# Two transformer blocks on one core: order of the hybrid layer's front and of the RWKV chunk queries

## The chip, the cores and the metric

The kernel runs on one NeuronCore of a Trainium2 chip. The metric is the device time of one execution in microseconds; the kernel before was timed three times, and one further execution was profiled.

## The reference

A first block of two layers and a second block of one layer work on 512 tokens of width 1024, with 256 context (later memory) rows beside them, all in float32. The change touches two places.

The first is the front of layer 0, the hybrid mixer:

```
mod = silu(c) @ ada_w + ada_b                      # six blocks of 1024 per layer
hx = rms_norm(x) * (1 + sc1) + sh1;  hc the same with the context's shift and scale
p = h @ w_in                                       # q, k, v, z, xbc, dt for 512 + 256 rows
q, k = rope(rms_norm(q)), rope(rms_norm(k))        # the context's k is not rotated
a = softmax(q k^T / 8) v                           # 8 heads, 2 key heads, 768 keys
xbc = silu(conv3(xbc) + conv_b)                    # 768 channels, width 3 along the tokens
dt = softplus(p_dt + bias);  y = ssd scan(xbc, dt) in both directions
out = [a, rms_norm(y * silu(z))] @ w_out
```

The second is the RWKV-7 recurrence of the second block, 16 heads of 64, which the kernel computes in chunks of 64 tokens: a chunk's transition matrix G and its own state H, the states S(c+1) = G S(c) + H, and the rows read from a state with the chunk's queries RQ.

## The kernel before

The program is one stream of instructions for each engine, written out by hand. Streams are tied by semaphores: a `Progress` object names the steps of one stream, `done("x")` is the count at which step x is over. Activations lie channel by partition: X, HX and the others hold 8 tiles of 128 channels by 512 tokens, the context's 256 behind them. Weights come as units of 512 KB through a ring of four slots that SyncE fills in one fixed order: it asks for unit u + 4 once TensorE has freed unit u. The `ada_w` rows go through four slots of their own (AW). The order of the streams decides everything around the change; no planner is involved.

The front of layer 0 runs so:

- VectorE sums the first two ada blocks (lines 2387 and 2398), TensorE adds them over the partitions (line 1131). VectorE norms the latent tiles (`norm_dve`, lines 778 and 787), then those of the context, then makes MOD, MODC and both GAINs (lines 2411 to 2415). ScalarE waits for the last of these, "gainc", and writes the latent and the context tiles of HX (line 684).
- Projections: for four query pairs and the key TensorE makes product, square sum (line 1171) and rope swap (line 1176), ScalarE copy, square and root, VectorE reciprocal and rotation (lines 2447 to 2455), and between them the first 12 ada units (line 2429). The value unit gives tokens by channels (line 1191).
- Attention: 16 steps g, four query tiles for each of four head pairs. TensorE's order in a step is `scores(g + 1)` (lines 1229, 1231), three eighths of a fill (line 1265), block sums of ada where a block has ended (line 1253), six transposes of head 0 (line 1242), two eighths of the fill, six transposes of head 1, the last three eighths, and behind each fourth step `values` (line 1280). A fill is one projection unit that attention doesn't need: z0 to z3, then xbc tile by tile, latent (512 columns) and context (256). ScalarE has `exps(g + 1)` (line 2057), two transposed copies (line 2070) and the fill's copy (line 2079). VectorE has `weights(g)` (lines 2491, 2493), `row_max(g + 1)` (line 2484) and five ada units, three in a step with a context fill.
- Tail: after the last values and the last block sum's MOD, VectorE convolves six tiles of 770 columns (lines 2517, 2520) into two buffers by turns, ScalarE takes SiLU of z (line 2085) and of each convolved tile (lines 2089, 2090), then exponential and logarithm for dt; TensorE transposes the convolved tiles (line 1306), VectorE makes dt (lines 2528 to 2556) and copies (line 2562). GpSimd fetches the B and C rows by DMA once the last tile is out. The scan over four head pairs follows.

In the RWKV part eight passes run, one for each head pair (`pair_pass`). After the inverse of a chunk TensorE makes the products for the queries ("rq", line 1648), the transitions ("gt", line 1653) and the states ("h", lines 1658, 1661). VectorE adds bonus (line 2890), queries (2893), transitions in two halves (2897), states (2901) and copies the first state (2904). Then six transitions follow, each one TensorE product (1680) and one VectorE step (2907), with products of the next pair's projections in between (1507).

Of the kernel before, what the change touches and what calls it, by code (L numbers as in the profile page):

```python
# [8 lines left out]
ALU = mybir.AluOpType  # L9
# [48 lines left out]
FILLS = [("z", j, U_Z + j) for j in range(NPAIR)] + [(part, j, U_X + j) for j in range(XBC_TILES) for part in ("lat", "ctx")]  # L58
# [4 lines left out]
for _kind, _, _ in FILLS:  # L63
    ADA_UPTO.append(ADA_UPTO[-1] + (3 if _kind == "ctx" else 5))
# [224 lines left out]
def two_blocks(nc, a, consts_d, bias_d, out):  # L289

    ctx = ExitStack()
    with ctx:
# [98 lines left out]
        t_cv = arena(low + 12900)  # L391
        CONV = t_cv(2, TA + 2)
# [85 lines left out]
        ada_dve = prog("ada_dve", "mod modc gain gainc")  # L478
        norm_lat, norm_ctx = NormStage(prog, "norm_lat", True), NormStage(prog, "norm_ctx", True)
        hy_act = prog("hy_act", "q0 sq0 q1 sq1 root0 k ksq root1 q2 sq2 kroot q3 sq3 root2 root3")  # L480
# [7 lines left out]
        at_act = prog("at_act", "exp00 exp01 " + by_step(lambda g: (f"exp{g + 1}0 exp{g + 1}1 " if g + 1 < STEPS else "") + f"pt{g}0 pt{g}1 e{g}"  # L488
# [43 lines left out]
        for steps, ahead in ((rw_steps, True), (rz_steps, False)):  # L532
            def next_pair(names):
# [4 lines left out]
                           + " w rq gt h s1 s2 yp s3 s4 s5 s6 y" + next_pair("lora") + "mean var")  # L538
# [7 lines left out]
                            + next_pair("nmax ninv nk") + "bv rq gt0 gt1 dh st1 s1 s2 s3 s4 s5 s6" + next_pair("d2 m2") + "ys yc"  # L546
# [320 lines left out]
        def _(sp):  # L867
# [257 lines left out]
        def _(pe):  # L1125
# [90 lines left out]
            nc.tensor.matmul(bank[4], const["rope_swap"], KT[:, 0:T], start=True, stop=True).then_inc(hy_pe.sem, hy_pe.step("kswap"))  # L1216
            swapped(2)
# [298 lines left out]
            def pair_pass(i, at, p_pe, p_act, p_dve, p_pool, ahead):  # L1516
# [129 lines left out]
                for t, c, e in quads:  # L1646
                    own = halves[c]
                    mm = nc.tensor.matmul(bank[2 + c][halves[e], t * CHUNK:(t + 1) * CHUNK], W21[own, 4 * e + t, 0, :], GR[own, 4 * e + t, 1, :], start=True, stop=True)
                mm.then_inc(p_pe.sem, p_pe.step("rq"))

                for t, c, e in quads:
                    own = halves[c]
# [9 lines left out]
                mm.then_inc(p_pe.sem, p_pe.step("h"))  # L1662

# [327 lines left out]
        def _(act):  # L1991
# [55 lines left out]
            query_root(2, "krstd")  # L2047
            query_root(3, "rstd2")
# [13 lines left out]
            for g in range(STEPS):  # L2062
# [13 lines left out]
                else:  # L2076
                    act.wait_ge(freed[ring.slot("hy_in", u)], ring.used("hy_in", u))
                    dst, src = (ZS[:, j, :], bank[7]) if kind == "z" else (XB[:, j, T + 3:TA + 3], bank[7][:, 0:TC])
                nc.scalar.activation(dst, src, ACT.Copy).then_inc(at_act.sem, at_act.step(f"e{g}"))
# [1045 lines left out]
```

## Time and profile before

| | us |
|---|---|
| median of the three timed runs | 2965.5 |
| the runs | 2955.92, 2965.5, 2968.95 |
| profiled execution, its own time | 2954.55 |
| its span | 2952.6 |
| TensorE matmul busy | 2752.6 (93%) |
| VectorE busy | 1709.6 (58%) |
| ScalarE busy | 645.8 (22%) |
| GpSimd busy | 188.5 (6%) |
| chain that ended last | TensorE 86%, VectorE 8%, issue 3% |
| mean granted clock of TensorE | 0.968 |

The span is the time from the first to the last recorded instruction; the execution's own time holds some 2 us more. The granted clock is a share of 2.4 GHz, so 0.50 is 1.2 GHz. Matmuls in float32 are recorded twice, so that one product of 128 by 512 shows as two records of 0.43 us.

### The profile page before, as it was taken

The numbers are of one execution on the slowest core, as the hardware profiler recorded it, in microseconds if no ns is written. First come the engines' busy times: TensorE is split into PE (matmuls) and PEld (weight loads), VectorE is DVE, ScalarE is ACT, GpSimd is POOL, SyncE is SP. The second block draws the span as 40 slices with busy tenths as digits, with TensorE's granted clock in tenths as the row PEclk, the third lists the DMA queues.
The fourth block names the chain that finished last, engine by engine and source line by source line (L and its number), as shares of the span: only waits on it lengthen the run. The fifth ranks groups of instructions, "written<-read, shape, count | busy, mean of one in ns | idle before, by whom it ended". The sixth has DMA issues, their size and how long they took to land.

```text
span 2952.6 us, 42986 instructions
## 1 busy us (share of the span) xinstructions
PE 2752.6 (93%) x17241; PEld 2007.0 (68%) x17241; DVE 1709.6 (58%) x2286; ACT 645.8 (22%) x1089; POOL 188.5 (6%) x203
## 2 busy tenths in 40 slices
PE   4799787999999999999989999998989999999998
PEld 3455443788887878888655555565557788788887
DVE  7677775655547665554456555663345575655554
ACT  3133412211101021110132223321341121211002
POOL 2000121000010010000030000010000010100001
PEclk8999898999999999999999999998999999999999
DMA  7466401333332323333211111111203333223332
GB/s 237 127 209 207 125 11 43 92 96 88 98 99 81 97 78 99 92 92 97 74 34 32 42 46 34 37 37 47 59 24 92 96 90 112 84 87 100 93 98 72
DMA packets 393989, 255.46 MB, mean 87 GB/s; under 512 B 19879, under 2 KB 376832, under 8 KB 393728
## 3 DMA queue, kind: packets, MB, share of 16 engines
q1 hardware_dynamic: 390256, 243.63, 28.0%
q0 software_dynamic: 2320, 5.11, 0.6%
q10 hardware_dynamic: 1280, 4.78, 0.4%
q8 instruction: 103, 1.69, 0.2%
q14 instruction: 30, 0.25, 0.0%
HBM read 250.60 MB, written 2.10 MB: 86 GB/s over the span
## 4 chain that ended last, share of the span: by engine, by line
PE 86%; DVE 8%; issue 3%; ACT 1%; DVEq 0%; DMA 0%; POOL 0%; ACTq 0%; SPq 0%; POOLq 0%
PE PS L827 14%; PE PS L826 14%; PE PS L828 14%; PE PS L1532 4%; PE PS L1507 3%; PE PS L841 3%; PE PS L842 3%; PE PS L843 3%; PE PS L813 3%; PE PS L1265 3%; PE PS L1598 1%; PE PS L1513 1%; PE PS L1624 1%; PE PS L1622 1%; PE PS L1718 1%
## 5 line engine op out<-in xcount | busy, mean ns | idle before, releaser
L852 DVE CAST WH<-W 128x1024 fp32r<-128x1024 f32 x304 | 213.3, 702 | 417.7 <-PE PS L828 371.9
L827 PE MATMUL PS<-XNL,WH 128*128 128x512 f32 x960 | 382.0, 398 | 0.0
L854 DVE TENSOR_TENSOR WL<-W,WH 128x1024 fp32r<-128x1024 f32 x304 | 374.5, 1232 | 10.4
L826 PE MATMUL PS<-HH,WH 128*128 128x512 f32 x672 | 262.3, 390 | 0.1
L827 PE MATMUL PS<-HL,WH 128*128 128x512 f32 x672 | 261.7, 389 | 0.0
L828 PE MATMUL PS<-HH,WL 128*128 128x512 f32 x672 | 261.7, 389 | 0.0
L827 PEld LDWEIGHTS PS<-XNL,WH 128*128 128x128 f32 x960 | 181.0, 189 | 41.5 <-issue 0.5
L828 PE MATMUL PS<-XNH,WL 128*128 128x512 f32 x512 | 201.7, 394 | 0.0
L826 PE MATMUL PS<-XNH,WH 128*128 128x512 f32 x512 | 201.2, 393 | 0.0
L826 PE MATMUL PS<-XN2H,WH 128*128 128x512 f32 x448 | 178.7, 399 | 10.7 <-issue 6.8
L828 PE MATMUL PS<-XN2H,WL 128*128 128x512 f32 x448 | 177.7, 397 | 0.0
L1532 PE MATMUL PS<-HXF,W 128*128 128x512 f32 x336 | 165.4, 618 | 0.0
L841 PE MATMUL PS<-XNH,WH 128*128 128x512 f32 x384 | 154.7, 403 | 9.9 <-DVE XNL L768 9.9
L842 PE MATMUL PS<-XNL,WH 128*128 128x512 f32 x384 | 154.9, 403 | 0.0
L843 PE MATMUL PS<-XNH,WL 128*128 128x512 f32 x384 | 153.6, 400 | 0.0
L826 PEld LDWEIGHTS PS<-HH,WH 128*128 128x128 f32 x672 | 126.1, 188 | 27.9 <-DVE HL L3092 1.3
L828 PEld LDWEIGHTS PS<-HH,WL 128*128 128x128 f32 x672 | 126.2, 188 | 26.4
L827 PEld LDWEIGHTS PS<-HL,WH 128*128 128x128 f32 x672 | 126.2, 188 | 26.1
L2880 DVE TENSOR_TENSOR ARENA<-ARENA,PS 128x512 f32<-128x512 f32 (+1 forms) x80 | 50.8, 635 | 140.2 <-PE PS L1624 139.9
L826 PEld LDWEIGHTS PS<-XNH,WH 128*128 128x128 f32 x512 | 96.4, 188 | 23.6 <-issue 0.2
L828 PEld LDWEIGHTS PS<-XNH,WL 128*128 128x128 f32 x512 | 96.2, 188 | 21.9
L826 PEld LDWEIGHTS PS<-XN2H,WH 128*128 128x128 f32 x448 | 85.1, 190 | 34.6 <-issue 14.7
(499 smaller groups left out, 4727.3 us busy)
## 6 DMA issues: line engine op xcount, KB each, us to landing
ARENA<-in_ada_w SPq DMA_DIRECT2D x80, 512.0 KB, 4.9
W<-in_ffn_w SPq DMA_DIRECT2D x64, 512.0 KB, 3.8
W<-in_w_in SPq DMA_DIRECT2D x51, 512.0 KB, 4.1
W<-in_ffn_w_gate SPq DMA_DIRECT2D x44, 512.0 KB, 3.8
W<-in_ffn_w_up SPq DMA_DIRECT2D x44, 512.0 KB, 3.8
W<-in_ffn_w_down SPq DMA_DIRECT2D x32, 512.0 KB, 3.7
W<-in_sc_w_in SPq DMA_DIRECT2D x24, 512.0 KB, 3.7
W<-in_ada_w SPq DMA_DIRECT2D x16, 512.0 KB, 4.7
```

Source lines behind the costliest of these rows:

```text
L813: mm = nc.tensor.matmul(dst, w[:, k, :], rhs(k), start=(start and k == 0), stop=(stop and k == kts - 1))
L826: nc.tensor.matmul(dst, WH[:, h, c], hi(k), start=(start and k == 0), stop=False)
L827: nc.tensor.matmul(dst, WH[:, h, c], lo(k), start=False, stop=False)
L828: mm = nc.tensor.matmul(dst, WL[:, h, c], hi(k), start=False, stop=(stop and k == kts - 1))
L841: nc.tensor.matmul(dst[u], WH[:, h, c], hi(k), start=(k == 0), stop=False)
L842: nc.tensor.matmul(dst[u], WH[:, h, c], lo(k), start=False, stop=False)
L843: mm = nc.tensor.matmul(dst[u], WL[:, h, c], hi(k), start=False, stop=(k == KD - 1))
L852: nc.vector.tensor_copy(WH[:, h, :], W[:, s, 0:D]).then_inc(parted, 1)
L854: nc.vector.tensor_tensor(WL[:, h, :], W[:, s, 0:D], WH[:, h, :], ALU.subtract).then_inc(freed[s], 1)
L1265: mm = nc.tensor.matmul(bank[7][:, 0:n], tiles(s)[:, k, :], (cx if kind == "ctx" else lat)(k), start=(k == 0), stop=(k == KD - 1))
L1507: return nc.tensor.matmul(bank[7], w, xn(k), start=(k == 0), stop=(k == KD - 1))
L1532: mm = nc.tensor.matmul(bank[7], tiles(s)[:, k, :], xn(k), start=(k == 0), stop=(k == KD - 1))
```

## The change

- The latent MOD and GAIN are made ahead of the context's norm, and ScalarE's latent outputs wait for that gain alone; the context's MODC and GAIN follow, then the context's norm.
- The first z unit is multiplied within the projections, behind the key's swap, into bank 2; ScalarE copies it out ahead of the last root. The list of fills begins with z1, all fills move up by one step, and step 15 has none. The first three eighths of step 0's fill stand ahead of `scores(1)`.
- The convolution of tile j runs on VectorE in step 5 + 2j, behind the maximum of the next step and ahead of the ada units. It writes into a buffer of its own (tile 0) or into the part of XB that tile j - 1 has left. These odd steps have three ada units, the others five; these were also the steps with three before.
- After attention ScalarE waits for the last MOD, takes SiLU of the six convolved tiles, and then SiLU of z.
- In each RWKV pair the "rq" matmuls go behind "h", and the add into RQ behind the copy of the first state.

```diff
-FILLS = [("z", j, U_Z + j) for j in range(NPAIR)] + [(part, j, U_X + j) for j in range(XBC_TILES) for part in ("lat", "ctx")]
+FILLS = ([("z", j, U_Z + j) for j in range(1, NPAIR)] + [(part, j, U_X + j) for j in range(XBC_TILES) for part in ("lat", "ctx")]
+         + [(None, None, None)])
+CONV_STEP = {5 + 2 * j: j for j in range(XBC_TILES)}
...
-for _kind, _, _ in FILLS:
-    ADA_UPTO.append(ADA_UPTO[-1] + (3 if _kind == "ctx" else 5))
+for _g in range(STEPS):
+    ADA_UPTO.append(ADA_UPTO[-1] + (3 if _g in CONV_STEP else 5))
...
-        t_cv = arena(low + 12900)
-        CONV = t_cv(2, TA + 2)
+        CONV = [t_hy(TA + 2)] + [XB[:, j, 0:TA + 2] for j in range(XBC_TILES - 1)]
...
         SyncE, per step: the z and ctx units of FILLS[g - 1] ask for unit u + 4
-                for u in [SLOTS + u for kind, _, u in FILLS[max(g - 1, 0):g] if kind != "lat" and SLOTS + u < 16]:
+                for u in [SLOTS + u for kind, _, u in (FILLS[g - 1:g] if g else [("z", 0, U_Z)]) if kind in ("z", "ctx") and SLOTS + u < 16]:
...
         TensorE, after the key's swap
+            s = ring.slot("hy_in", U_Z)
+            pe.wait_ge(hy_act.sem, hy_act.done("sq2"))
+            pe.wait_ge(landed[s], ring.arrived("hy_in", U_Z))
+            unit_product(pe, "hy_in", U_Z, 0, bank[2], lat, KD).then_inc(freed[s], 1)
             swapped(2)
...
         TensorE, fill(g, ks)
+                if kind is None:
+                    return
...
+                    else:
+                        pe.wait_ge(hy_dve.sem, hy_dve.done("sin3"))
...
             pe.wait_ge(hy_dve.sem, hy_dve.done("dt"))
+            pe.wait_ge(hy_act.sem, hy_act.done("z0"))
             scores(0)
             for g in range(STEPS):
+                if g == 0:
+                    fill(g, range(0, 3))
                 if g + 1 < STEPS:
                     scores(g + 1)
-                fill(g, range(0, 3))
+                if g:
+                    fill(g, range(0, 3))
...
         TensorE, RWKV pair: the rq loop (its four lines unchanged) goes from ahead of gt to behind h
...
         ScalarE
+            act.wait_ge(ada_dve.sem, ada_dve.done("gain"))
+            norm_act_out(act, norm_lat, HX[:, :, 0:T], GAIN[:, 0, :], MOD[:, 0:KD])
             act.wait_ge(ada_dve.sem, ada_dve.done("gainc"))
-            norm_act_out(act, norm_lat, HX[:, :, 0:T], GAIN[:, 0, :], MOD[:, 0:KD])
             norm_act_out(act, norm_ctx, HX[:, :, T:TA], GAIN[:, 1, :], MODC[:, 0:KD])
...
             query_root(2, "krstd")
+            act.wait_ge(freed[ring.slot("hy_in", U_Z)], ring.used("hy_in", U_Z))
+            nc.scalar.activation(ZS[:, 0, :], bank[2], ACT.Copy).then_inc(hy_act.sem, hy_act.step("z0"))
             query_root(3, "rstd2")
...
-            act.wait_ge(at_act.sem, at_act.done(f"e{NPAIR - 1}"))
-            nc.scalar.activation(ZS, ZS, ACT.Silu).then_inc(zs_act.sem, zs_act.step("silu"))
             act.wait_ge(at_dve.sem, at_dve.done(f"p{STEPS - 1}1"))
+            act.wait_ge(blocks_dve.sem, blocks_dve.done(f"b{len(ADA_BLOCKS) - 1}"))
             for j in range(XBC_TILES):
                 act.wait_ge(cv_dve.sem, cv_dve.done(f"c{j}"))
                 (the two Silu activations read CONV[j] instead of CONV[:, j % 2])
+            act.wait_ge(at_act.sem, at_act.done(f"e{NPAIR - 2}"))
+            nc.scalar.activation(ZS, ZS, ACT.Silu).then_inc(zs_act.sem, zs_act.step("silu"))
...
         VectorE
             norm_dve(dve, norm_lat, X, HX[:, :, 0:T], T)
             dve.wait_ge(norm_lat.dve.sem, norm_lat.dve.done(f"n{KD - 1}"))
-            norm_dve(dve, norm_ctx, CX, HX[:, :, T:TA], TC)
...
+            for m, at, name, step in ((MOD, 0, "mod", "gain"), (MODC, 4 * N_MOD, "modc", "gainc")):
+                nc.vector.tensor_tensor(m[:, 0:16], two(at, 16), adab(0, 16), ALU.add).then_inc(ada_dve.sem, ada_dve.step(name))
+                dve.wait_ge(ada_dve.sem, ada_dve.done(name))
+                nc.vector.scalar_tensor_tensor(GAIN[:, 0 if m is MOD else 1, :], m[:, KD:2 * KD], 1.0, cols_of("norm_mix", 0, KD), ALU.add, ALU.mult).then_inc(ada_dve.sem, ada_dve.step(step))
+            norm_dve(dve, norm_ctx, CX, HX[:, :, T:TA], TC)
...
+            def convolution(j):
+
+                dve.wait_ge(at_act.sem, at_act.done(f"e{4 + 2 * j}"))
+                out_ = CONV[j]
+                (the loop over "abc" as it was; from j = 2 on a waits for c of tile j - 1)
...
             for g in range(STEPS):
                 weights(g)
                 if g + 1 < STEPS:
                     row_max(g + 1)
+                if g in CONV_STEP:
+                    convolution(CONV_STEP[g])
                 for n in range(ADA_UPTO[g], ADA_UPTO[g + 1]):
                     ada_unit(n)
...
-            dve.wait_ge(at_pe.sem, at_pe.done(f"pv{NPAIR - 1}"))
-            dve.wait_ge(at_act.sem, at_act.done(f"e{STEPS - 1}"))
-            for j in range(XBC_TILES):
-                (wait for ScalarE's silu of tile j - 2, then the loop over "abc" into CONV[:, j % 2])
...
         VectorE, RWKV pair: the wait for rq and the add into RQ go from behind bv to behind st1
```


## Rows read from the trace of the kernel before

**Rows 1.** The page, part 1: busy us, share, instructions of each engine.
```profile
PE 2752.6 (93%) x17241; PEld 2007.0 (68%) x17241; DVE 1709.6 (58%) x2286; ACT 645.8 (22%) x1089; POOL 188.5 (6%) x203
```

**Rows 2.** Busy time by stretch; columns: stretch, length, five engines, TensorE clock, DMA.
```profile
60.00:66.00 6.00, 0.00 (x0) 0.00 (x0) 5.46 (x17) 0.45 (x1) 0.00 (x0) 0.50 0.20 79
336.50:353.70 17.20, 0.03 (x1) 0.03 (x1) 16.25 (x23) 7.90 (x14) 0.00 (x0) 0.58 0.00 0
```

**Rows 3.** Timeline, norms to query 0; columns: start us, length, instruction, idle time before, releaser.
```profile
60.51 1.75 DVE L778 RECIPROCAL RSTD<-ROOT 128x256 f32<-128x256 f32 x1
...
65.55 5.75 ACT L684 ACTIVATE HXF<-HXF,MOD,GAIN 128x512 f32<-128x512 f32 x8 [9.51 <-DVE GAIN L2415]
...
66.50 15.42 PE L813 MATMUL PS<-HXF,W 128*128 128x512 f32 x32 [7.13 <-ACT HXF L684]
```

**Rows 4.** Timeline of SyncE and TensorE, late projections.
```profile
108.03 0.43 SPq L891 DMA_DIRECT2D W<-in_hy_w_in  x1
...
129.53 2.07 PE L1176 MATMUL PS<-ARENA,CONST 128*128 128x512 f32 x2 [8.80 <-DVE ARENA L2449]
```

**Rows 5.** Timeline of TensorE, first steps of attention.
```profile
152.29 2.08 PE L1229 MATMUL PS<-ARENA 64*128 64x512 f32 x4 [4.30 <-ACT ARENA L2057]
...
155.15 4.33 PE L1265 MATMUL PS<-HXF,W 128*128 128x512 f32 x6
```

**Rows 6.** Timeline of TensorE, then VectorE, steps 8 to 10 of attention.
```profile
260.05 1.13 PE L1229 MATMUL PS<-ARENA 64*128 64x512 f32 x4
...
265.36 0.85 PE L1242 MATMUL PS<-CONST,ARENA 128*128 128x128 f32 x6 [0.74 <-ACT ARENA L2070]
...
267.43 1.13 PE L1229 MATMUL PS<-ARENA 64*128 64x512 f32 x4
...
279.04 1.13 PE L1229 MATMUL PS<-ARENA 64*128 64x512 f32 x4
...
250.05 1.82 DVE L2484 TENSOR_REDUCE ARENA<-PS 128x1 f32<-128x768 f32 x2 [5.44 <-PE PS L1231]
...
263.39 4.05 DVE L2429 SCALAR_TENSOR_TENSOR ARENA<-ARENA,SILU_C 128x1024 f32<-128x1024 f32 x3
...
267.56 0.62 DVE L2493 TENSOR_SCALAR ARENA<-ARENA 128x768 f32<-128x768 f32 x1
```

**Rows 7.** Timeline of the tail: TensorE, VectorE, ScalarE.
```profile
328.38 5.37 PE L1280 MATMUL PS<-ARENA 128*64 128x512 f32 x24
334.44 1.95 PE L1253 MATMUL PS<-CONST,ARENA 128*128 128x2 f32 x16 [0.70 <-ACT ARENA L2082]
353.68 5.38 PE L1306 MATMUL PS<-CONST,ARENA 128*128 128x128 f32 x24 [17.28 <-ACT ARENA L2090]
...
336.51 0.62 DVE L2517 TENSOR_SCALAR ARENA<-ARENA,COLS 128x770 f32<-128x770 f32 x1
...
355.43 0.21 DVE L2536 TENSOR_SCALAR ARENA<-ARENA 128x96 f32<-128x96 f32 x1 [2.17 <-ACT ARENA L2096]
...
335.70 1.91 ACT L2085 ACTIVATE ARENA<-ARENA 128x2048 f32<-128x2048 f32 x1
...
352.50 0.72 ACT L2089 ACTIVATE ARENA<-ARENA,COLS 128x512 f32<-128x512 f32 x1 [1.52 <-DVE ARENA L2520]
353.13 0.49 ACT L2090 ACTIVATE ARENA<-ARENA,COLS 128x256 f32<-128x256 f32 x1
```

**Rows 8.** Timeline of the second RWKV pair: VectorE, then TensorE.
```profile
1624.06 0.69 DVE L2893 TENSOR_TENSOR ARENA<-PS,ARENA 128x512 f32<-128x512 f32 x1
1624.67 1.40 DVE L2897 TENSOR_TENSOR ARENA<-PS,CONST 64x512 f32<-64x512 f32 x2
...
1626.83 0.20 DVE L2904 COPY ARENA<-ARENA 128x64 f32<-128x64 f32 x1
...
1627.17 0.41 PE L1680 MATMUL PS<-ARENA 128*128 128x64 f32 x2 [1.77 <-DVE ARENA L2904]
...
1629.12 1.91 PE L1507 MATMUL PS<-HXF,W 128*128 128x512 f32 x2
```

More of the change, by code:

```diff
@@ L537, in two_blocks @@
                                       + (" akv" if l == 0 else "") for l in levels)
-                           + " w rq gt h s1 s2 yp s3 s4 s5 s6 y" + next_pair("lora") + "mean var")
+                           + " w gt h rq s1 s2 yp s3 s4 s5 s6 y" + next_pair("lora") + "mean var")
             steps["act"] = (("raw0" if ahead else "dila") + " tr0 tr1 tr2 tr3 "
@@ L1647, in pair_pass @@
                     own = halves[c]
[L1648 to L1652, printed above, removed]
                     mm = nc.tensor.matmul(bank[4 + c][halves[e], t * HEAD:(t + 1) * HEAD], W21[own, 4 * e + t, 0, :], TOK[own, t, 1, halves[e]], start=True, stop=True)
@@ L1662, in pair_pass @@
                 mm.then_inc(p_pe.sem, p_pe.step("h"))
+                for t, c, e in quads:
+                    own = halves[c]
+                    mm = nc.tensor.matmul(bank[2 + c][halves[e], t * CHUNK:(t + 1) * CHUNK], W21[own, 4 * e + t, 0, :], GR[own, 4 * e + t, 1, :], start=True, stop=True)
+                mm.then_inc(p_pe.sem, p_pe.step("rq"))
                 def inside_rows(tiles_of):
@@ L2410, in _ @@
             cols_of = lambda name, k, n: COLS[:, COL[name] + k:COL[name] + k + n]
-            nc.vector.tensor_tensor(MOD[:, 0:16], two(0, 16), adab(0, 16), ALU.add).then_inc(ada_dve.sem, ada_dve.step("mod"))
-            nc.vector.tensor_tensor(MODC[:, 0:16], two(4 * N_MOD, 16), adab(0, 16), ALU.add).then_inc(ada_dve.sem, ada_dve.step("modc"))
-            dve.wait_ge(ada_dve.sem, ada_dve.done("modc"))
-            for w, m in enumerate((MOD, MODC)):
-                nc.vector.scalar_tensor_tensor(GAIN[:, w, :], m[:, KD:2 * KD], 1.0, cols_of("norm_mix", 0, KD), ALU.add, ALU.mult).then_inc(ada_dve.sem, ada_dve.step(("gain", "gainc")[w]))
+            for m, at, name, step in ((MOD, 0, "mod", "gain"), (MODC, 4 * N_MOD, "modc", "gainc")):
[3 more added lines that the diff above has]
+            norm_dve(dve, norm_ctx, CX, HX[:, :, T:TA], TC)
             dve.wait_ge(norm_ctx.dve.sem, norm_ctx.dve.done(f"n{KD - 1}"))
@@ L2493, in weights @@
                     nc.vector.tensor_scalar(PR[g % 2][:, e, :], PR[g % 2][:, e, :], own, None, ALU.mult).then_inc(at_dve.sem, at_dve.step(f"p{g}{e}"))
+            def convolution(j):
+                dve.wait_ge(at_act.sem, at_act.done(f"e{4 + 2 * j}"))
+                out_ = CONV[j]
+                for w, step in enumerate("abc"):
+                    src, wcol = XB[:, j, w:w + TA + 2], col("conv_w", w * XBC_TILES + j)
+                    if w == 0:
+                        if j > 1:
+                            dve.wait_ge(cv_dve.sem, cv_dve.done(f"c{j - 1}"))
+                        ins = nc.vector.tensor_scalar(out_, src, wcol, None, ALU.mult)
+                    else:
+                        dve.wait_ge(cv_dve.sem, cv_dve.done(f"{'abc'[w - 1]}{j}"))
+                        ins = nc.vector.scalar_tensor_tensor(out_, src, wcol, out_, ALU.mult, ALU.add)
+                    ins.then_inc(cv_dve.sem, cv_dve.step(f"{step}{j}"))
             row_max(0)
@@ L2890, in pair_pass @@
                 tt(BV, bank[6], v, ALU.mult).then_inc(p_dve.sem, p_dve.step("bv"))
-                dve.wait_ge(p_pe.sem, p_pe.done("rq", at))
-                by_chunk = lambda ap: ap.rearrange("p t (c d) -> p t c d", c=2)
-                tt(by_chunk(RQ), chunk_pairs(2), by_chunk(AR[:, :, 1, :]), ALU.add).then_inc(p_dve.sem, p_dve.step("rq"))
                 dve.wait_ge(p_pe.sem, p_pe.done("gt", at))
@@ L2904, in pair_pass @@
                 nc.vector.tensor_copy(ST[:, 1, :], DH[:, 0, :]).then_inc(p_dve.sem, p_dve.step("st1"))
+                dve.wait_ge(p_pe.sem, p_pe.done("rq", at))
+                by_chunk = lambda ap: ap.rearrange("p t (c d) -> p t c d", c=2)
+                tt(by_chunk(RQ), chunk_pairs(2), by_chunk(AR[:, :, 1, :]), ALU.add).then_inc(p_dve.sem, p_dve.step("rq"))
                 for c in range(1, NCHUNK - 1):
```

28 lines of the change are left out of this document (9 added, 19 removed).

## The prediction

> **What bounds the kernel now.** I read the busy line first: TensorE is busy 93% of the span, VectorE 58% [rows 1]; the chain that ended last is TensorE's to 86%. So an edit pays only where TensorE stands idle and waits for the work that is moved, or where work leaves a stretch in which TensorE sets the pace. The table by stretches shows two such places at once: 60 to 66 us, no matmul, and 336.5 to 353.7 us, 17.2 us with one matmul, VectorE busy 16.25 us [rows 2]. The timelines then show what runs there, and three smaller gaps: 8.80 us ahead of the third query's swap, 4.30 us ahead of the second scores, and 1.77 us in each RWKV pair [rows 4, 5, 8]. One clock fact colours all: after an idle stretch TensorE comes back at a granted 0.50, that is 1.2 GHz; the same four score matmuls take 2.08 us then and 1.13 us at 2.4 GHz [rows 5, 6].
>
> The sum is made against the profiled execution, 2954.55 us (span 2952.6 and some 2 us around it). The three timed runs have their median at 2965.5, 11 us above it, so I subtract the same sum from the median.
>
> **A. Gain of the latent rows ahead of the context's norm.** Today the latent tiles are normed when the reciprocal of the context starts at 60.51; ScalarE's latent outputs start at 65.55, once the context's reciprocal, eight products and four small adds are through, and query 0 follows at 66.50 [rows 3]. In the new order MOD and GAIN (two small adds, some 0.35 us with their waits; TensorE's sums, their input, ended before 60 [rows 2]) stand directly at 60.51, so the outputs start at 60.9: 65.55 - 60.9 = 4.65 us. The context's norm then ends at 65.6 and its outputs go through ScalarE from 66.6 to 70.6; the key product that needs them comes after two queries (15.4 us from 61.85), at 78. Up to the first scores everything hangs on this chain of TensorE and VectorE, so all moves by **4.65**.
>
> **B. First z unit in the projections.** Sixteen matmul records of 0.43 us are 6.9 us. They stand between the key's swap (ends 129.53 - 8.80 = 120.7) and swap 2, which waits for VectorE until 129.53 [rows 4]: hidden, if the weights are there; SyncE asks for that unit at 108.03 [rows 4] and such 512 KB land in some 4 us. The copy by ScalarE (0.6 us) stands ahead of root 3, whose input comes later. If the cover were gone it would cost 6.9. The gap filled, swap 2 runs at 2.4 GHz: 2.07 becomes 1.1, and the next VectorE step waits for just it: **0.95** (bounds 0 and 0.95).
>
> **C. The fills move up by one.** (1) Step 0. The first three k of the fill (six records, 4.33 us at the low clock) now stand before scores 1 instead of behind, in the 4.30 us in which TensorE waits for the exponentials [rows 5]. They hide. Scores 1 then come after busy time: 3.0 us at the low clock become 1.5. Together 4.3 + 1.4 = **5.7** (4.3 if the clock stays low).
> (2) Full steps. From scores to scores a step with a 512-column fill takes 11.6 us with block sums (9.9 without their 1.7), one with a 256-column fill 7.4, of which 0.9 is waiting (8.2 without the wait and with block sums), values 5.3 [rows 6, 7]. Until now VectorE had three ada units (1.33 each) in the short steps; the trace shows TensorE waiting 0.74 us there for ScalarE's transposed copy, behind maximum and exponentials [rows 6]. Now the odd steps have the long fill, three units and a convolution (six take 336.51 to 352.4, 2.65 us each [rows 7]), the even ones five units, short fill and block sums. VectorE's pair, from start to next start: two weights of 1.44 (reciprocal and product, twice), two maxima of 1.74, eight units 10.1, mod 0.1, convolution 2.65: 19.25 us [rows 6, 7]. TensorE's pair: 9.9 + 8.3 = 18.2. VectorE lags, but the values (5.3 us, no VectorE work) let it catch up once in four steps. Walked through four steps with these durations, maximum g+1 starts 1.3 us late in the second step and 2.2 late in the fourth, and TensorE waits 0.1, 0.45 and 0.85 us for the copy: 1.4 in place of 1.8 (0.9 twice). Two such groups: **0.8** (bounds -5, if the pair's whole excess of 1 us is paid in five pairs, and 3.6, all waits gone).
> (3) Last four steps. Step 15 has no fill. TensorE's work is 6.9 us less, but the last pair is VectorE's: its weights come 29.6 us after scores 13, transposes and copies end at 32.7, values at 38.0, against 42.0 today. That is 4.0. Behind the last fill stand some 3 us of idle time and only transposes, and rows say what idle costs: values (5.37) and block sums (1.95) [rows 7] at 1.2 GHz would take up to 7 more. I take 3, left **1.0** (bounds -3 and 4).
>
> **D. Convolution out of the tail.** Today: last block sum taken over at 336.5, six convolutions to 352.4, last SiLU at 353.62, transposes at 353.68 [rows 7]. After: all convolutions lie in attention (the last in step 15, under values), and ScalarE starts when the last mod is there: table load 1.28, six times 1.03 (0.72 and 0.49 pipelined), so transposes 7.5 us after it instead of 17.2: 9.6. But SiLU of z (1.91) now stands behind them on the same engine, ahead of the dt exponentials. VectorE waits for that exponential even today, 2.17 us [rows 7]; it comes 1.9 later relative to the transposes. Its chain (dta, three copies) then reaches the C.B products at 8.6 us behind the last SiLU instead of 7.5. So 1.1 is given back: **8.5** (bounds 7.5 and 9.6). The B and C copies by DMA start when the last tile is out and are wanted 7 us later. What waits behind ScalarE's new wait for the last mod is only this work.
>
> **E. RWKV.** Today the chunk query matmuls (32 records, 0.52 us issue) and their add on VectorE (0.69, next start 0.61 later) lie before the transition adds; state 1 comes at 1626.83 and the first transition at 1627.17, TensorE idle 1.77 [rows 8]. Behind h the matmuls fall into that idle time, and the adds start with the transition at 1624.06, its products having been where the queries' were. State 1 comes 0.61 earlier. The query add then fills the 0.6 us in which VectorE waits for transition 1. From there TensorE is busy without a gap to the pair's end, so eight pairs give 8 x 0.61 = **4.9** (bounds 0 and 5).
> The clock there: in four of seven projecting pairs it falls to 1.2 GHz some 2 us behind that idle time (two records take 1.91 us [rows 8], elsewhere 1.08), and state 1 to y takes 10.6 instead of 8.96 us, 1.7 more. Idle time of 1.2 instead of 1.8 us may spare some or none: I take one, **1.7** (bounds -5, dips in all seven, and 6.8, none).
> The Trainium skill, "TensorE: Matmul & The Clock Gate", part "A second HAM failure mode: psum-queue depth-cycling", says that small idle times between groups of matmuls are enough to make the clock swing. The trace agrees (four of seven). By it alone, fewer idle times mean fewer dips, 6.8 for E in place of 1.7; and against C it speaks, as the last rival does.
>
> **Sum.** 4.65 + 0.95 + 5.7 + 0.8 + 1.0 + 8.5 + 4.9 + 1.7 = 28.2. Profiled execution 2926.3; median 2965.5 - 28.2 = 2937.
>
> **Rivals.**
> 1. VectorE becomes the bound of attention. For: 19.25 against 18.2 us a pair, and ScalarE between them. Against: VectorE stands idle 5.44 us at each values [rows 6]. If the five convolutions beside fills are paid in full, 5 x 2.65 = 13.3 lost: 2950.
> 2. The idle stretches are not removed but refilled: a later link (weights of an earlier asked unit, the dt chain on ScalarE, scores 0) sets the pace, and of A to D, 21.6 us, half is seen: 2948. For: each gap has a second releaser close behind (dt chain 1.1). Against: those that I could follow come later only by what is subtracted.
> 3. More: no dip in RWKV and values at the full clock: 28.2 + 5.1 + 3 = 36: 2929.
> 4. Slower. The waits for VectorE in steps 5 to 14 grow until the clock falls to 1.2 GHz in every step. Ten steps have 83 us of matmul time at 2.4 GHz and as much again at 1.2: 2937 + 83 = 3020, half of it 2978. It decides from idle times about as long as the 1.77 us after which RWKV shows dips; I come to 0.85. That swing of the clock is what the named page of the Trainium skill speaks of.
>
> **Chances.** Forecast 0.60, rival 3 0.15, rival 1 0.10, rival 2 0.10, rival 4 0.05. Leaving out rival 4 and the far ends, and with 5 us for the spread of the runs, the range is 2918 to 2955. A measurement of this kernel can tell some 0.5%, 15 us, from no change. Faster by more than that (below 2950.7): forecast and rival 3 nearly whole, half of 1 and 2: 0.83. Within: 0.13. Slower: 0.04.
>
> **What would show it.** Latent outputs near 60.9; no idle time ahead of swap 2; scores 1 under 2 us and at the old wait's end; the wait for the transposed copy under 1 us in steps 5 to 14; values 3 at 5.3 or up to 10.6 us; transposes 7.5 us after the last mod; first transition 1.2 us after h in every pair. Wrong would make it: the clock below 1.0 between steps 2 and 14, or VectorE busy without a gap through the values.

## The result and the profile after

| | before | after |
|---|---|---|
| median of the runs, us | 2966.25 (4 runs) | 2934.94 (4 runs) |
| profiled execution, us (span) | 2954.55 (2952.6) | 2924.85 (2922.9) |
| mean granted clock of that execution | 0.968 | 0.971 |

The ratio of the times, changed to before, is 0.9907, 95% interval 0.9889 to 0.9925: 22 to 33 us less. The forecast was 28.2 us less and a median of 2937. In the page of the changed kernel, TensorE's busy time hardly moves against [rows 1]; what went is idle time.

```profile
PE 2748.7 (94%) x17241; PEld 2005.4 (69%) x17241; DVE 1707.1 (58%) x2286; ACT 644.9 (22%) x1089; POOL 187.1 (6%) x203
```

The timelines of the changed kernel answer to the rows in their order (start, length, instruction, idle time before it and its releaser). The front, ScalarE and then TensorE, answers to [rows 3, 4]: the latent outputs start at 61.05 instead of 65.55, query 0 at 62.01 instead of 66.50, and swap 2 takes 1.18 instead of 2.07 us, with 1.94 us of idle time ahead of it instead of 8.80.

```profile
61.05 5.75 ACT L685 ACTIVATE HXF<-HXF,MOD,GAIN 128x512 f32<-128x512 f32 x8 [4.87 <-DVE GAIN L2430]
...
62.01 16.68 PE L814 MATMUL PS<-HXF,W 128*128 128x512 f32 x32 [2.50 <-ACT HXF L685]
...
101.55 1.86 PE L1209 MATMUL PS<-ARENA,CONST 128*128 128x512 f32 x2
...
119.00 7.03 PE L814 MATMUL PS<-HXF,W 128*128 128x512 f32 x16
127.97 1.18 PE L1177 MATMUL PS<-ARENA,CONST 128*128 128x512 f32 x2 [1.94 <-DVE ARENA L2464]
```

TensorE in attention answers to [rows 5 to 7]: the fill of step 0 stands ahead of the second scores (149.85), which now run at 2.4 GHz (1.13 instead of 2.08 us). In the middle the longest wait for the transposed copy is 0.62 us, where it was 0.74. In the last step, now without a fill, waits of 2.67, 0.99 and 0.95 us stand ahead of both groups of transposes and of values 3, which takes 6.99 instead of 5.37 us.

```profile
145.48 3.07 PE L1274 MATMUL PS<-HXF,W 128*128 128x512 f32 x6
149.85 1.13 PE L1234 MATMUL PS<-ARENA 64*128 64x512 f32 x4 [1.31 <-ACT ARENA L2072]
150.82 0.60 PE L1236 MATMUL PS<-ARENA 64*128 64x256 f32 x4
151.34 1.95 PE L1258 MATMUL PS<-CONST,ARENA 128*128 128x2 f32 x16
...
264.73 0.85 PE L1247 MATMUL PS<-CONST,ARENA 128*128 128x128 f32 x6 [0.18 <-ACT ARENA L2085]
...
274.13 0.85 PE L1247 MATMUL PS<-CONST,ARENA 128*128 128x128 f32 x6 [0.62 <-ACT ARENA L2085]
...
312.43 0.88 PE L1247 MATMUL PS<-CONST,ARENA 128*128 128x128 f32 x6 [2.67 <-DVE ARENA L2508]
...
314.29 1.51 PE L1247 MATMUL PS<-CONST,ARENA 128*128 128x128 f32 x6 [0.99 <-ACT ARENA L2085]
316.75 6.99 PE L1289 MATMUL PS<-ARENA 128*64 128x512 f32 x24 [0.95 <-issue]
324.43 1.95 PE L1258 MATMUL PS<-CONST,ARENA 128*128 128x2 f32 x16 [0.69 <-ACT ARENA L2098]
```

The tail (TensorE, VectorE, ScalarE) answers to [rows 7]. The transposes of the convolved rows wait 7.79 us instead of 17.28, and now for ScalarE's SiLUs alone. The SiLU of z (334.02) stands behind them, and VectorE waits 10.36 us for ScalarE's exponential, which comes after it.

```profile
334.16 4.26 PE L1319 MATMUL PS<-CONST,ARENA 128*128 128x128 f32 x24 [7.79 <-ACT ARENA L2105]
...
346.23 3.78 PE L1372 MATMUL PS<-ARENA,CONST 128*128 128x512 f32 x4 [1.39 <-ACT ARENA L2124]
...
326.41 0.17 DVE L2455 TENSOR_TENSOR MOD<-PS,COLS 128x8 f32<-128x8 f32 x1 [6.70 <-PE PS L1258]
...
337.72 0.21 DVE L2553 TENSOR_SCALAR ARENA<-ARENA 128x96 f32<-128x96 f32 x1 [10.36 <-ACT ARENA L2113]
...
326.64 1.28 ACT L2104 ACT_TABLE_LOAD   x1 [2.27 <-DVE MOD L2455]
...
333.62 0.49 ACT L2105 ACTIVATE ARENA<-ARENA,COLS 128x256 f32<-128x256 f32 x1
334.02 1.90 ACT L2107 ACTIVATE ARENA<-ARENA 128x2048 f32<-128x2048 f32 x1
```

The second RWKV pass, VectorE and then TensorE, answers to [rows 8]: the query add stands behind the copy of state 1, the idle time ahead of the first transition is 1.17 instead of 1.77 us, and the first late projection takes 1.12 instead of 1.91. From state 1 to the next pass's state 1 it is 65.45 us in each of the first six passes; before it was 66.05 or 67.7. A pass in which the clock falls to 1.2 GHz behind the idle time, and state 1 to y takes longer for it, is called one with a dip below.

```profile
1605.69 0.20 DVE L2918 COPY ARENA<-ARENA 128x64 f32<-128x64 f32 x1
1605.80 0.69 DVE L2921 TENSOR_TENSOR ARENA<-PS,ARENA 128x512 f32<-128x512 f32 x1
...
1606.03 0.41 PE L1692 MATMUL PS<-ARENA 128*128 128x64 f32 x2 [1.17 <-DVE ARENA L2918]
...
1607.99 1.12 PE L1520 MATMUL PS<-HXF,W 128*128 128x512 f32 x2
```

### The profile page after: what moved, and what is told of

It reads as the page before. It is cut to its first block, busy times and chain, and to the rows that moved or that the text cites. A ratio compares the mean times of both kernels' runs of the same rounds, so it can differ in the third digit from the quotient of the medians.

```text
span 2922.9 us, 42991 instructions
## 1 busy us (share of the span) xinstructions
PE 2748.7 (94%) x17241; PEld 2005.4 (69%) x17241; DVE 1707.1 (58%) x2286; ACT 644.9 (22%) x1089; POOL 187.1 (6%) x203
## 4 chain that ended last, share of the span: by engine, by line
PE 83%; DVE 9%; issue 4%; ACT 2%; POOL 1%; DMA 1%; DVEq 0%; ACTq 0%; POOLq 0%; SPq 0%
PE PS L828 14%; PE PS L827 14%; PE PS L829 14%; PE PS L1545 4%; PE PS L1520 3%; PE PS L843 3%; PE PS L842 3%; PE PS L844 3%; PE PS L814 2%; DVE ARENA L2444 2%; PE PS L1611 2%; PE PS L1637 1%; PE PS L1526 1%; PE PS L1635 1%; PE PS L1274 1%
## 5 line engine op out<-in xcount | busy, mean ns | idle before, releaser
L855 DVE TENSOR_TENSOR WL<-W,WH 128x1024 fp32r<-128x1024 f32 x304 | 374.5, 1232 | 10.4
```

The lines of the kernel that those rows point to most:

```text
L855: nc.vector.tensor_tensor(WL[:, h, :], W[:, s, 0:D], WH[:, h, :], ALU.subtract).then_inc(freed[s], 1)
```

## The experiments

The study is told in the order of its questions. Letters are the prediction's terms. Runs of one kernel spread over 3 to 16 us, so each comparison has a time and a place in the trace. Ratios are to the kernel before, run beside the version, with a 95% interval in brackets.

**RWKV order alone** (the kernel before, with part E and nothing else):

```
TensorE's order, then VectorE's
- " w rq gt h s1 s2 ..."
+ " w gt h rq s1 s2 ..."
- "bv rq gt0 gt1 dh st1 s1 ..."
+ "bv gt0 gt1 dh st1 rq s1 ..."
```

> The kernel before with the RWKV reorder alone. First theory (the sum's term E): TensorE's idle time ahead of the first transition goes from 1.77 to 1.17 us in each of eight passes, 8 x 0.61 = 4.9 us, and with the shorter idle time the clock falls in fewer of the seven projecting passes than the four of before, down to none as in the changed kernel's profile, up to 6.8 us more: passes 65.45 us apart throughout, time 5 to 12 us under the kernel before, ratio 0.996 to 0.998. Rival: the falls of the clock belong to the execution and not to the idle time; then some passes still stand 67.1 us apart, and the gain is 4.9 us, ratio 0.998.

Measured: 2948.03 us, median of 10 runs; ratio 0.9966 [0.9952, 0.9981], 6 to 14 us less, 10 in the middle. The idle time ahead of the first transition is 1.17 or 1.18 us in each pass, as in the changed kernel:

```profile
1629.96 0.41 PE L1679 MATMUL PS<-ARENA 128*128 128x64 f32 x2 [1.18 <-DVE ARENA L2900]
```

State 1 to y took 10.65 us in one of seven projecting passes and 8.96 to 9.13 in the others; in the kernel before it was four of seven. So E is worth about 10 us, more than the 6.6 taken, and the excess is the dips. The rival, that they belong to the execution and not to the idle time, needs the count over all profiles, further on.

**Front alone** (the changed kernel with RWKV's old order, the reverse of the diff above):

> The changed kernel with the RWKV part as before (queries ahead of the transitions in both streams). First theory: all of A to D stays, some 18 to 21 us under the kernel before (ratio 0.993 to 0.994), the idle time in RWKV is 1.77 us again and some passes show the clock at 1.2 GHz, so passes stand 66.06 or 67.7 us apart. Rival (the falls of the clock belong to the execution): passes all 66.06 us apart may come as often as not; then the profile shows no dip although the idle time is 1.77 us.

Measured: 2944.14 us; ratio 0.9957 [0.9941, 0.9974], 8 to 17 us less. Five of seven passes have the dip, with 1.77 us of idle time as before. The two halves, 10.1 and 12.7 us, sum to 22.8 against 27.5 for both; the intervals allow that they simply add. The front alone came out below its expectation and below the trace (19 us, in the table further on); its own runs go from 2937.2, the profiled one, to 2947.1, and why three of four were longer by 5 to 10 us no trace shows.

**Latent gain first, alone** (the kernel before, with part A):

```
- norm_dve(dve, norm_ctx, ...)      (stood ahead of both gains)
+ mod gain modc gainc, then norm_dve(dve, norm_ctx, ...)
```

> The kernel before with term A alone, the latent gain ahead of the context's norm. First theory: the latent outputs start 4.5 us earlier (65.55 to 61.05) and everything behind shifts rigidly, so scores 0 come at 140.6 instead of 145.06, ratio 0.9985. Rival, from the changed kernel's profile, where scores 0 came only 2.4 us earlier: the head start is partly paid back by stretches at 1.2 GHz in the projections (query 0 and the key's square sums), whose place moves with the start, so scores 0 come at 142 to 143.5 and the ratio is 0.999.

Measured: 2952.74 us (10 runs); ratio 0.9980 [0.9970, 0.9990], 3 to 9 us less. In its trace query 0 came at 61.83 (4.67 us earlier than [rows 3]), but the first scores at 143.28 against 145.06, 1.8 us earlier, as the rival said. A second trace of the kernel before shows how much of that gap is chance:

**The kernel before, once more**

> The kernel before, unchanged, for a second profile. Its first scores stood at 145.06 us in the first one. The versions with the changed front put them at 142.4 to 142.8 in four profiles and at 139.3 and 139.9 in two, with a granted clock from 60 to 80 us of 0.81 to 0.82 in the late and 0.87 to 0.88 in the early ones. Theory that the gap is scatter of the clock and not of the change: this profile has the scores at 142 to 143 or at 145, whichever, and dips in 3 to 5 of its seven full RWKV passes. Rival, that the change itself brings the low stretches at 66 to 120 us: 145.06 again within 0.3.

Measured: 2969.54 us (one run), first scores at 147.36, dips in five of seven. This is neither of the two places that the expectation named: the first profile's 145.06 was itself early (the RWKV-only kernel, with the same front, had 147.37). The key's square sums tell the two kinds of execution apart. In the first profile of before the longer of them ran at 2.4 GHz (1.02 us):

```profile
104.81 1.02 PE L1208 MATMUL PS<-ARENA,CONST 128*128 128x512 f32 x2
```

In the second it ran at 1.2 GHz (1.91):

```profile
105.87 1.91 PE L1208 MATMUL PS<-ARENA,CONST 128*128 128x512 f32 x2
...
147.36 2.08 PE L1229 MATMUL PS<-ARENA 64*128 64x512 f32 x4 [2.80 <-DVE ARENA L2475]
```

In the version with A alone it did so too:

```profile
101.33 1.92 PE L1208 MATMUL PS<-ARENA,CONST 128*128 128x512 f32 x2
...
143.28 2.08 PE L1229 MATMUL PS<-ARENA 64*128 64x512 f32 x4 [2.80 <-DVE ARENA L2474]
```

Like against like, A is worth 4.1 us at the first scores (147.36 - 143.28), near the 4.65 taken. Most of what seemed given back was the kind of execution that the first profile of before happened to be.

**Fill of step 0 behind the second scores again** (C1 undone):

```
-                if g == 0:
-                    fill(g, range(0, 3))
                 if g + 1 < STEPS:
                     scores(g + 1)
-                if g:
-                    fill(g, range(0, 3))
+                fill(g, range(0, 3))
```

> The changed kernel with the fill of attention step 0 put back behind the scores of step 1 (the term C1 undone; it was 5.7 us in the two traces, 3.1 of it the fill itself). My theory: the first block sums come 5 to 6 us later and so does every marker behind them, 5 to 6 us in the end (2940 to 2941). Rival: the fill itself is off the path, since the scores of step 1 wait for their PSUM anyway (idle 1.31 us ahead of them now): then 1.3 us of it comes back and the loss is about 4.3 us. Second rival: the 5.7 us came from the shorter scores (full instead of low clock in step 1) and not from the order; then the loss is under 2 us.

Measured: 2942.17 us, 6.5 above the 2935.6 that is the median of all ten runs of the changed kernel; its four runs go from 2932 to 2945, so it is the trace that decides. TensorE's timeline of step 0 gives the old picture back: 4.31 us of idle time, scores of 2.08 us, and the fill behind them.

```profile
142.40 2.08 PE L1234 MATMUL PS<-ARENA 64*128 64x512 f32 x4 [2.80 <-DVE ARENA L2487]
...
149.64 2.08 PE L1234 MATMUL PS<-ARENA 64*128 64x512 f32 x4 [4.31 <-ACT ARENA L2069]
...
152.50 4.24 PE L1274 MATMUL PS<-HXF,W 128*128 128x512 f32 x6
156.57 1.84 PE L1258 MATMUL PS<-CONST,ARENA 128*128 128x2 f32 x16
```

The block sums stand 14.17 us behind the first scores, in the changed kernel 8.72: 5.45. Both rivals, 4.3 and under 2, are out in the trace. (The expectation's 5.7 for the two traces is 5.54 by the starts of the block sums, see C1 below.)

**Convolutions behind the last modulation again** (D undone), run twice, the second time beside the changed kernel itself:

```
-                if g in CONV_STEP:
-                    convolution(CONV_STEP[g])
...
+            for j in range(XBC_TILES):
+                convolution(j)
```

> The changed kernel with the six convolution groups of the hybrid's attention put back behind the last modulation matmul, as before (the convolution's own term, D, undone; everything else as changed). My theory (D = 9.6 us off the tail, 1.1 us given back by a scan start that waits for the output gate): TensorE's tail transposes start about 17 to 18 us after the last MOD group instead of 7.8 us, and the kernel takes 8 to 10 us longer than the changed one (2943 to 2945, about 0.994 of before). Rival: the convolution had been hidden behind the last attention step in the old order as well (its matmuls fill idle time of TensorE there): then under 3 us longer. Second rival: with fewer matmuls in the last steps the clock is lower there and values 3 takes 8.2 instead of 7.0 us, which would add 1.2 us to the first.

> The changed kernel, unchanged, timed beside the next two. Scatter theory: its median lies at 2928 to 2937 and its first scores at 139.5 or at 142.6; no dip, or one, in the seven full RWKV passes (gaps of 65.45 us). It is the mark for the next two kernels.

> The kernel with the convolutions back behind the last modulation, again. In its first profile the tail's transposes stood 199.2 us behind the first scores against 191.5 in the changed kernel (7.6 us), but its median (2934.2) was no longer than that of the changed kernel (2934.9), measured in another call. Theory (the 7.6 us are real and scatter in the clock hid them): beside the changed kernel on one chip it takes 6 to 9 us more (0.2 to 0.3 per cent). Rival (given back later, in the scan, in the feed-forward layer or by the clock): no difference over 2 us.

Measured: first 2934.18 us (4 runs), as fast as the changed kernel's 2934.94, which was not run beside it. Side by side it took 2944.47 against 2935.77 (6 runs each; ratios 0.9936 [0.9919, 0.9952] and 0.9914 [0.9898, 0.9931]): 8.7 us by the medians, 6.5 by the ratios. Over all, ten runs each, the means are 2939.3 and 2934.2: 5.1 us, with a standard error of 2.5. By the times alone the part is only just clear of the spread; the traces say where it lies. The changed kernel's own second profile had its first scores at 142.55, as expected, but two dips where none or one was. TensorE, then VectorE, in the first trace of the version without the change:

```profile
306.93 0.88 PE L1247 MATMUL PS<-CONST,ARENA 128*128 128x128 f32 x6 [1.86 <-DVE ARENA L2508]
...
310.58 7.01 PE L1289 MATMUL PS<-ARENA 128*64 128x512 f32 x24 [0.95 <-issue]
318.28 1.95 PE L1258 MATMUL PS<-CONST,ARENA 128*128 128x2 f32 x16 [0.69 <-ACT ARENA L2098]
338.51 4.15 PE L1319 MATMUL PS<-CONST,ARENA 128*128 128x128 f32 x24 [18.27 <-ACT ARENA L2105]
...
335.22 2.08 DVE L2522 SCALAR_TENSOR_TENSOR ARENA<-ARENA,COLS 128x770 f32<-128x770 f32 x2
```

The idle time ahead of the transposes is 18.27 us against 7.79: the tail pays 10.5. But its first scores stood at 139.33, so its last block sums came 178.95 us behind them, against 181.81 in the changed kernel: without convolutions between VectorE's maxima, attention is 2.9 us shorter. There no wait for a transposed copy is left until the last step, and the wait for the last weights is 1.86 us instead of 2.67. Net 7.6 in this trace, 4.4 in the second, where values 3 took 5.37 against 7.89. The second rival (a longer values 3) was not seen: 7.01 and 5.37 us.

**More idle time in RWKV** (the changed kernel; VectorE's query add ahead of the transition adds, while TensorE's queries stay behind h):

```
- "bv gt0 gt1 dh st1 rq s1 ..."
+ "bv rq gt0 gt1 dh st1 s1 ..."
```

> The changed kernel with VectorE's query add back ahead of the transition adds, TensorE's query matmuls left behind h. VectorE now waits for the late matmuls, so the first state comes some 1.3 us later than in the kernel before and TensorE stands idle some 3.1 us ahead of the first transition. First theory: idle time decides the dips, so most or all of the seven passes show 1.2 GHz behind it (1.7 us each), passes some 69 us apart: against the changed kernel 8 x 1.9 + up to 7 x 1.7 = 15 to 27 us more, ratio to the kernel before 0.995 to 0.999. Rival (idle time doesn't decide): 15 us more than the changed kernel and no more than four dips, ratio 0.995 to 0.997 with passes 67.4 us apart mostly.

Measured: 2966.74 us; ratio 1.0025 [1.0009, 1.0042]. One of its six runs took 3563 us at a mean granted clock of 0.737 (0.962 to 0.964 in the others); the ratio leaves it out, it has no trace, and nothing here has a reason for it. TensorE's timeline:

```profile
1614.65 0.41 PE L1692 MATMUL PS<-ARENA 128*128 128x64 f32 x2 [3.17 <-DVE ARENA L2921]
...
1617.35 2.07 PE L1520 MATMUL PS<-HXF,W 128*128 128x512 f32 x2
```

The idle time is 3.17 us in each pass, and all seven have the dip (state 1 to y 10.5 to 12.2 us). Against the changed kernel's median of 2935.6 that is 31 us more, beyond the 15 to 27 expected: from the first state 1 to the eighth it is 30.3, of which 7 x 2.0 are the idle time and 16 are dips, up to 3.3 us each instead of 1.7. The rival (no more than four dips) is out.

**SiLU early** (a version meant to beat both; run twice). ScalarE loads the SiLU table right behind its last transposed copy and does SiLU of z and four convolved tiles there, two more behind the last output copy; nothing of it waits for the last modulation any more, only for the last use of the weights that lay where the tiles go.

```
+                if g == STEPS - 1:
+                    nc.scalar.activation(ZS, ZS, ACT.Silu)...
+                    for u in range(AW_SLOTS):
+                        act.wait_ge(aw_used[u], ADA_UNITS // AW_SLOTS)
+                    for j in range(4):
+                        conv_silu(j)
-            act.wait_ge(blocks_dve.sem, ...)
-            for j in range(XBC_TILES): ... (both SiLUs of tile j)
+            for j in range(4, XBC_TILES):
+                conv_silu(j)
```

> A version meant to go beyond the changed kernel: ScalarE runs the SiLU of z and of the first four convolution tiles right behind its last exponential and ahead of the last output copy, with the table load there, instead of behind the last modulation; the convolution groups are already there by then. In the changed kernel 7.75 us lie between the last MOD group's start (326.41) and the tail's transposes (334.16), and the transposes wait for the SiLU in that time. Theory: the transposes then start at about 326.7 to 328, 6 to 7.5 us earlier, the scan start no longer waits for the output gate (1.1 us), and the kernel takes 6 to 8.5 us less than the changed one (2926.5 to 2929). Rival: the copies that ScalarE owes to the attention's end come later by the table load and five SiLUs (about 1.3 + 6 us) and the last modulation with them, so that the gain is 0 to 2 us.

> The kernel with the SiLU early, again, with more rounds. In its first profile the tail's transposes stood 184.4 us behind the first scores against 191.5 (7.1 us), the start of hybrid output 321.6 us behind them against 323.8 (2.2 us only), and its median was 11.9 us below the changed kernel's of another call. Theory (7.1 us stay): 6 to 9 us less than the changed kernel in this call. Rival (5 us of them are given back ahead of the hybrid's output, by low clock or by a later wait in the scan): 1.5 to 3 us less.

Measured: 2923.06 us (4 runs), then 2927.62 (4 runs) beside the changed kernel's 2935.77; ratios to before 0.9866 [0.984, 0.9892] and 0.989 [0.9875, 0.9906]. Side by side that is 8.1 us less by the medians, 7.1 by the ratios. The timeline of TensorE in its first trace:

```profile
314.04 7.28 PE L1289 MATMUL PS<-ARENA 128*64 128x512 f32 x24 [0.95 <-issue]
322.00 1.95 PE L1258 MATMUL PS<-CONST,ARENA 128*128 128x2 f32 x16 [0.69 <-ACT ARENA L2112]
324.30 4.48 PE L1319 MATMUL PS<-CONST,ARENA 128*128 128x128 f32 x24 [0.35 <-DVE MOD L2463]
```

The wait of 7.79 us is 0.35, and the output copy that ScalarE owes is no later. The 7.4 us stay, and the rival (5 of them given back) is out. Its 2923.06 us is the lowest median of the study, though the next version is not told apart from it. Its first trace was only 2.2 us ahead at the hybrid's output: its stretch from the transposes to there took 137.22 us at a granted clock of 0.87, against 132.25 at 0.90, see the spread below.

**SiLU early and a fill of z in the last step** (the z unit taken from the third step, later fills up by one):

```
- FILLS = z1 z2 z3, 12 units of x, none
+ FILLS = z1 z2, 12 units of x, none, z3
  (each convolution waits for the fill one step earlier)
```

> As the kernel before in this call (SiLU early), and a projection unit of z moved from an early attention step to the last one as a fill, so that TensorE has matmuls beside its transposes there. Theory (values 3 took 6.99 us at the low clock in the changed kernel, 5.37 in the kernel before, where such matmuls stood there): values 3 takes 5.4 us and the transposes of the last step run without the low clock, 1.6 to 3 us less than with the SiLU early alone. Rival: the fill takes 2.1 to 3.1 us of TensorE's own time in a step where TensorE sets the end, and the sum is nought or a loss of 1 us; the SiLU of z waits for it as well.

Measured: 2927.11 us, against 2923.06 for the version before, run beside it; ratio 0.9885 [0.9857, 0.9914], so not told apart. TensorE:

```profile
303.98 1.92 PE L1258 MATMUL PS<-CONST,ARENA 128*128 128x2 f32 x16 [1.24 <-DVE ARENA L2452]
...
308.91 1.51 PE L1247 MATMUL PS<-CONST,ARENA 128*128 128x128 f32 x6 [1.91 <-ACT ARENA L2091]
...
319.83 5.37 PE L1289 MATMUL PS<-ARENA 128*64 128x512 f32 x24
```

Values 3 is at 2.4 GHz as expected. But the transposes stand 188.0 us behind the first scores, against 184.4 and 185.3: the step without a fill is now the last but one and waits there, and the fill costs its own time. The rival holds, with 2.7 to 3.6 us lost up to there where it named 1 at most; the total shows no more than that nothing is gained.

## Why the prediction was right, and where its terms were off

Each kernel's profile is cut at four places: the first scores, the tail's first transposes, the first matmul of hybrid output, the end. As several kernels share each stretch unchanged, means over them take out much of the chance (all in us; old order, then as changed; n is the number of profiles).

| stretch | old | changed | gain | forecast |
|---|---|---|---|---|
| start to first scores | 146.60 (n 3) | 142.04 (n 10) | 4.6 | A + B = 5.6 |
| first scores to transposes | 208.33 (n 4) | 192.21 (n 4) | 16.1 | C1 + C2 + C3 + 9.6 = 17.1 |
| transposes to hybrid output | 133.09 (n 4) | 134.43 (n 4) | -1.3 | -1.1 |
| hybrid output to the end | 2468.85 (n 4) | 2459.41 (n 9) | 9.4 | E = 6.6 |
| sum | | | 28.8 | 28.2 |

The forecast is right in its mechanism and near in its number; how near is partly luck, since misses of 1 to 3 us cancel. In the prediction's working some roundings are off by 0.1 us (a pair of TensorE's steps is 9.9 + 8.2, 17.2 - 7.5 is 9.7), and nothing hangs on them.

**A and B.** The mechanism held: query 0 4.49 us earlier (4.65 forecast), swap 2 0.89 shorter (0.95). The z unit's 7.03 us lie in the old gap; no run has B alone, so B is read from the traces. In the first pair of traces the scores gained 2.4 us only, since queries 0 and 1 took 1.3 us longer, and 1.7 us went in the key's two square sums and the product behind them, at 1.2 GHz from 101.6 us. But that pair compares unlike executions. Those sums ran at 1.2 GHz in nine of the eleven profiles with the new front and in two of the three with the old. Where they did, the first scores went from 147.37 to 142.65 us (two and eight profiles with both A and B), 4.7 less; where they did not, from 145.06 to 139.6 (one and two), 5.4 less. So of 5.6 forecast 0.2 to 0.9 is missing; all profiles together, mixed as they came, give 1.0.

**C1.** 5.7 forecast; 5.54 in the first pair of traces, and 5.45 with only this undone. The first block sums came 7.98 us earlier, of which 2.44 are the first scores'. They start at 151.34 in the changed kernel, and in the kernel before:

```profile
159.32 1.84 PE L1253 MATMUL PS<-CONST,ARENA 128*128 128x2 f32 x16
```

**C2.** 0.8 forecast, 1.1 found (values 0 7.87 us earlier, values 2 8.95). The undoing of D shows it to be a difference of two larger sizes: the convolutions cost 1.4 us up to values 2 and 2.9 to the last block sums, so the rest of the change there gives 2.5 up to values 2. That it is the ada units, now three beside a long fill and five beside a short one, is argued and not shown: no run moved them alone. Rival 1, VectorE as the bound with 13.3 us lost, is refuted as a size and real as a mechanism. Rival 4 is refuted: from 160 to 320 us the granted clock is 0.98 to 1.00 in the ten traces compared.

**C3.** 1.0 forecast and 1.1 found in the first pair (the last block sums 10.01 us earlier), with 1.6 of the 3 us set aside for the low clock in values 3. That clock is chance: values 3 took from 5.37 to 8.21 us, and two profiles of one kernel gave 6.99 and 7.89, 7.01 and 5.37, 7.28 and 5.37. All lie within the bounds, none at the far one of 10.6.

**D.** Transposes 7.79 us behind the last modulation's sums (7.5 forecast, 17.28 before), 1.1 given back behind it (the products at 346.23 stand 12.07 us behind the transposes, before it was 10.92). Right in the pair of traces. As a price of the part by itself 8.5 was too high, since C2 paid 2.9 of it: undone alone, it is 4.4 to 7.6 us in the traces.

**E.** The term that was mis-sized. "I take one" dip less; in fact nearly all went. Over all profiles the dips in the seven projecting passes are these:

| idle time ahead of the first transition | profiles | passes with the dip |
|---|---|---|
| 1.17 us (new order) | 9 | 4 of 63 |
| 1.77 us (old order) | 4 | 19 of 28 |
| 3.17 us (add ahead, queries behind) | 1 | 7 of 7 |

From the first state 1 to the eighth, the old order takes 468.2 us and the new one 457.8, 10.4 less (four and nine profiles). Behind the eighth 1.2 us is given back. "From there TensorE is busy without a gap" holds for seven passes only: the eighth has no late projections, and TensorE waits 0.38 us ahead of each transition from the fourth on, in either order. But the query add costs nothing there: the first transition step starts 0.79 us behind the copy of state 1 in either order. What differs is the clock of the y product. It took 1.97 us in eight of the nine profiles of the new order:

```profile
2003.05 1.97 PE L1703 MATMUL PS<-ARENA 64*64 64x64 f32 x32 [0.38 <-DVE ARENA L2924]
```

In the ninth, the RWKV-only kernel, it took 1.15, as in three of four of the old order:

```profile
2027.84 1.15 PE L1690 MATMUL PS<-ARENA 64*64 64x64 f32 x32 [0.38 <-DVE ARENA L2906]
```

That accounts for 0.5 of the 1.2 us by the means; the rest lies behind y, and its cause is open. The Trainium skill, "TensorE: Matmul & The Clock Gate", part "A second HAM failure mode: psum-queue depth-cycling", says of another kernel that small idle times between its groups of matmuls make the clock swing. The trace agrees, and by it alone E would have been 4.9 + 6.8 = 11.7, against 9.4 measured; no row of before could tell how fast the swing vanishes between 1.77 and 1.17 us.

So 28.2 was near because E was 3 us too small while A with B, and C with D, were 1 us too large each. Rival 2 (gaps refilled, half the gain of 21.6) is refuted by the first three stretches, which give 19.4; rival 3 was half right, in its dips but not in values at the full clock.

**The spread.** The same instructions of the scan, from the transposes to hybrid output, in windows (stretch, length, busy time of TensorE, its weight loads, VectorE, ScalarE, GpSimd, then granted clock, DMA share and GB/s): the kernel before twice, and the version with convolutions behind twice.

```profile
353.68:483.99 130.31, 101.30 (x461) 58.73 (x461) 97.77 (x240) 29.72 (x53) 25.63 (x24) 0.91 0.05 15
```

```profile
355.55:494.73 139.18, 109.46 (x461) 63.16 (x461) 97.78 (x240) 29.74 (x53) 26.06 (x24) 0.86 0.05 14
```

```profile
338.51:470.28 131.77, 101.46 (x461) 57.79 (x461) 97.26 (x240) 31.37 (x54) 24.67 (x24) 0.90 0.05 15
```

```profile
340.30:483.35 143.05, 111.68 (x460) 64.19 (x461) 97.53 (x240) 31.38 (x54) 25.89 (x24) 0.83 0.05 13
```

VectorE's time is the same to 0.5 us, TensorE's is 8 to 10 us apart with the clock at 0.83 to 0.86 against 0.90 to 0.91, and the stretch 9 to 11 us. The difference in this one stretch is most of a kernel's spread between runs, and as large as the largest single terms here. In the old and the new order alike it fell either way, so the term of -1.1 is not confirmed by its mean.

## What to carry to other kernels

An idle gap of TensorE is worth what the next releaser leaves of it: follow the second and the third one, and fill it with matmuls that stand behind it anyway (step 0: 5.5 us). Where work moves onto an engine that keeps pace with TensorE, its price is paid in many small waits elsewhere; undo the part alone to see it. Before a part of 5 us is judged, cut two or more profiles at fixed instructions, since the clock in an unchanged stretch can move the total by 10, and compare only profiles in which the same instructions ran at the low clock.

## What the runs showed of the hardware that was not expected

- The swing of the clock in the RWKV passes depends steeply on one short idle time: 4 of 63 passes at 1.17 us, 19 of 28 at 1.77. The order of TensorE's work was changed with it; but from 1.17 to 3.17 us (7 of 7) that order was kept and only VectorE's moved. At 1.77 us no profile has two passes in a row without a dip, so the passes of one execution should not be counted as independent draws.
- A step with only transposes and small gaps leaves values 3 at the low clock for anything from none of it (5.37 us) to most of it (8.21).
- The scan's stretch ran in two profiles of one and the same kernel at a granted clock of 0.91 and 0.86 (before), 0.90 and 0.87 (changed), 0.90 and 0.83 (convolutions behind) and 0.87 and 0.84 (SiLU early), 3 to 11 us apart.
